# A feed-forward product as seven half-size block products, with the weight sums formed in DRAM

## The chip, the core and the metric

The kernel runs on one core of one Trainium2 chip. Its time is the device time of one execution, in microseconds (us). Names used below: TensorE is PE, VectorE is DVE, ScalarE is ACT, GpSimd is POOL, SyncE is SP. SP issues the weight loads (the hardware queue q1), GpSimd issues the transfers that copy or add from DRAM to DRAM (the software queue q0). All transfers run on the same 16 DMA engines.

## What is computed

One layer of a decoder with D_MODEL = 1024, 512 tokens and D_FF = 2816, all in float32. The parts that matter here:

```python
x = x + rms_norm(merged @ w_out[l], post_mix_g[l])
h = rms_norm(x, pre_ffn_g[l])
gt, up = jnp.split(h @ w_ffn_in[l], 2, axis=-1)      # the first product: (512,1024) @ (1024,5632)
f = (jax.nn.silu(gt) * up) @ w_ffn_out[l]            # the second: (512,2816) @ (2816,1024)
x = x + rms_norm(f, post_ffn_g[l])
```

Before it stand a combined input projection, attention, a pooling mixer and a convolution, whose gated sum is `merged` (the mix).

## The kernel before

Each float32 operand is split into a rounded part (hi, float32r) and the rest (lo), and each product is three matmuls: hi x hi, hi x lo, lo x hi (`mm3`, L1291 to L1295). A "unit" is what one 512 KB weight load feeds. SP loads it into one of three slots of `raw` (L285, L289), once DVE has split the unit three before it. ACT writes `w_hi` (L506; L778 in the second product) once PE has done the unit three before it, DVE writes `w_lo` (L814; L1239), and PE waits for `lo_done`. So every engine goes through the units in one fixed order, written out by hand, and whatever stands between two splits on ACT or DVE delays the next split.

The stages in order of time: the projection with attention (units of 24 matmuls of 512 columns); eight mix units; the output product (`out_tile`, L1472) with the norms and transposes; the first product of the feed-forward part; the second product.

Mix: for each of 8 tiles DVE applies the gates (L1082), GpSimd adds the three branches (L462, L463) for tiles 0 to 6, DVE does it for tile 7 (L1088, L1091), ACT and DVE split the sum (`merged_hi` L674, `merged_lo` L1066). DVE then splits the output weights (`wo_lo_part`). `out_tile(0, 0)` and `out_tile(0, 1)` take steps 0 to 5 first and then steps 6 and 7, each step waiting for its split tile and weights.

First product: 22 tiles of 128 hidden columns, in 11 pairs (tile s and tile s + 11), each tile with a gate unit and an up unit, 44 units (`ff_unit` L1523). The first three units run as two halves of 256 tokens, that is 256 columns a matmul. ACT takes the tanh (L744), DVE makes silu and the product (L1158, L1169, L1175, L1177), and DVE forms for each pair the sums s1 to s4 (L1172 to L1185) that the second product wants.

Second product: it runs as Winograd's form of Strassen's method, seven half-size products in the place of eight (`PH_P1` ... `PH_P4`), in 39 units of 12 matmuls of 512 columns. Four of the seven take sums of weight blocks. GpSimd forms these in DRAM (`combine` L440), a copy and then transfers with an add on landing (L436 and L438), each waiting for the one before it: chunks 0 to 2 early (after the pooling sums), chunks 3 to 5 after the norms. GpSimd's order is: pooling sums, 24 transfers, a power for the layer norm (L457), the mix adds, the norms' reciprocal roots (L467, L391, L395), 24 transfers, the final roots.

Of the kernel before, what the change touches and what calls it, by code (L numbers as in the profile page):

```python
# [29 lines left out]
P = 128  # L30
SEQ = 512
# [25 lines left out]
U_DOWN = U_FF + 2 * FF_TILES  # L57
FF_HALF = FF_TILES // 2
RING = 3
# [9 lines left out]
COMB_STEPS = 8 * COMB_CHUNKS  # L69
DOWN_SPLIT = (PH_P5, PH_P6, PH_P3, PH_P7, PH_P4)  # L70

# [41 lines left out]
def build(nc, x, w_in, w_branch, w_out, w_ffn_in, w_ffn_out, vecs, post_mix_g, pre_ffn_g, post_ffn_g,  # L113
          rel_bias, w_pool_g, onehot, pool_const, out):
    comb = nc.dram_tensor("comb", (4, FF_HALF * P, SEQ), F32, kind="Internal").ap()
    bias_scratch = nc.dram_tensor("bias_scratch", (2 * PAIRS, BIAS_LEN), F32, kind="Internal").ap()
# [54 lines left out]

    a11_hi = at("a11_hi", 68, [FF_HALF, TOK_HALF], F32R)
    a11_lo = at("a11_lo", 79, [FF_HALF, TOK_HALF], F32R)
    a12_hi = at("a12_hi", 90, [FF_HALF, TOK_HALF], F32R)
    a12_lo = at("a12_lo", 101, [FF_HALF, TOK_HALF], F32R)
    s1 = at("s1", 112, [FF_HALF, TOK_HALF])
    s2 = at("s2", 123, [FF_HALF, TOK_HALF])
    s3 = at("s3", 134, [FF_HALF, TOK_HALF])
    s4 = at("s4", 145, [FF_HALF, TOK_HALF])
    n22 = at("n22", 168, [FF_HALF, TOK_HALF])  # L180
    ff_tanh = at("ff_tanh", 156, [2, SEQ])
    ff_silu = at("ff_silu", 160, [2, SEQ])
    ff_prod = at("ff_prod", 164, [2, SEQ])
# [3 lines left out]
    c22 = at("c22", 52, [2, SEQ])  # L187
    c12 = at("c12", 56, [2, SEQ])
    c21 = at("c21", 60, [2, SEQ])
# [16 lines left out]
    with ExitStack() as ctx:  # L206
        bank = [ctx.enter_context(nc.psum_tensor(f"bank{i}", [P, SEQ], F32)) for i in range(8)]

        def sem(name):
# [43 lines left out]
        comb_step, f_mix, s_hi_done, s_lo_done, p_moved, c_made = (  # L253
            sem("comb_step"), sem("f_mix"), sem("s_hi_done"), sem("s_lo_done"), sem("p_moved"), sem("c_made"))
# [7 lines left out]
        w_up_k = w_ffn_in[0].rearrange("(k p) n -> p k n", p=P)  # L262
# [21 lines left out]
        def _(sp):  # L284
# [52 lines left out]
            def ff_load(e, slot):  # L337

                s_, odd = divmod(e, 2)
                col = odd * DFF + (s_ // 2 + FF_HALF * (s_ % 2)) * P  # L340
                load(U_FF + e, slot, w_up_k[:, :, col:col + P], k8)

            for e in range(8):
                ff_load(e, (U_FF + e) % RING)
# [3 lines left out]
            with sp.Fori(0, 3) as i:  # L348
                for jj in range(12):
                    q = jj // 2  # L350
                    col = i * (3 * P) + (jj % 2) * DFF + (2 + q // 2 + FF_HALF * (q % 2)) * P
                    load(U_FF + 8 + i * 12 + jj, (U_FF + 8 + jj) % RING, w_up_k[:, :, bass.ds(col, P)], k8)
# [10 lines left out]
            for n in range(DOWN_UNITS):  # L363
                u = U_DOWN + n
                sp.wait_ge(lo_done, u - RING + 1)
                if n == 5:
                    sp.wait_ge(comb_step, 16 * COMB_STEPS)
# [13 lines left out]
        def _(pool):  # L381
# [45 lines left out]
            comb_count = 0  # L427

            def comb_dma(to, src, rows, add=False):

                nonlocal comb_count
                if comb_count:
                    pool.wait_ge(comb_step, 16 * comb_count)
                comb_count += 1
                if add:
                    pool.dma_start(comb[to, rows, :], src, accum_op=ALU.add).then_inc(comb_step, 16)  # L436
                else:
                    pool.dma_start(comb[to, rows, :], src).then_inc(comb_step, 16)  # L438

            def combine(c):  # L440
# [3 lines left out]
                comb_dma(0, w_ffn_out[0, rows, 0:SEQ], rows)  # L444
                comb_dma(0, w_ffn_out[0, rows, SEQ:], rows, add=True)
                comb_dma(1, comb[0, rows, :], rows)
                comb_dma(1, w_ffn_out[0, low, SEQ:], rows, add=True)
                comb_dma(2, w_ffn_out[0, low, SEQ:], rows)
                comb_dma(2, w_ffn_out[0, rows, SEQ:], rows, add=True)
                comb_dma(3, comb[1, rows, :], rows)  # L450
                comb_dma(3, w_ffn_out[0, low, 0:SEQ], rows, add=True)

            for c in range(3):
                combine(c)
# [3 lines left out]

            for m in range(KT - 1):
                b = m % 2  # L460
                pool.wait_ge(mix_read, m + 1)
# [3 lines left out]
            for t in range(TOK):  # L465
# [25 lines left out]
        def _(act):  # L491
# [254 lines left out]
            for e in range(8):  # L746
                if e >= 1:
                    hi_int(U_FF + 2 + e)
                if e % 2 == 0:
                    j = e // 2  # L750
                    if j:
                        f_hi_part((j - 1) // 2, (j - 1) % 2, j - 1)
                    ff_tanh_part(j, j % 2, FFB[e % 4])
            with act.Fori(0, 3) as i:
                for jj in range(12):
# [891 lines left out]
```

## Time and profile before

| | |
|---|---|
| median of 3 runs | 725.66 us (725.49 to 727.19) |
| profiled execution, its own time | 725.84 us |
| its span, first to last instruction | 724.0 us |
| granted PE clock, mean | 0.997 |
| PE busy | 707.5 us, 98% of the span |
| DVE, ACT, POOL busy | 434.9, 300.6, 88.2 us |
| DMA queues q1 and q0, share of 16 engines | 38.1% and 15.7% |

A busy PE means that a matmul is in flight; matmuls overlap (one of 512 columns is shown 390 ns long and the next starts 227 ns later), so the pace is read from the starts. "Idle before" is the time an engine stood still before an instruction, and the name behind the arrow is what ended it. A DMA is followed from its issue to its landing.

### The profile page before, as it was taken

What the parts mean: (1) busy time and instruction counts of PE and PEld (TensorE: products, weight loads), DVE (VectorE), ACT (ScalarE), POOL (GpSimd) and SP (SyncE); (2) the same over time, 40 slices, a digit from 0 to 9 for tenths busy, and PEclk for the clock granted to TensorE, in tenths of its full rate; (3) what the DMA queues carried; (4) which work ended last, traced back from release to release, by engine and by line L of the source; (5) the groups of instructions that cost most, each with busy time, mean ns of one, the idle gap of its engine ahead of it and who ended that gap; (6) DMA issues with size and microseconds to landing.
All of it is one profiled execution on the core that took longest, in us unless ns stands there. A gap on an engine that the chain in (4) does not pass through costs nothing.

```text
span 724.0 us, 9407 instructions
## 1 busy us (share of the span) xinstructions
PE 707.5 (98%) x3296; PEld 590.6 (82%) x3296; DVE 434.9 (60%) x693; ACT 300.6 (42%) x483; POOL 88.2 (12%) x115
## 2 busy tenths in 40 slices
PE   4999999999999999999999999999999999999996
PEld 4788888888888888888889888888888888888885
DVE  5427868578666575786565445444445444666767
ACT  6324544544455555242443222222222222566653
POOL 2032111111000000760221111111000000000003
PEclk9999999999999999999999999999999999999998
DMA  8436777877623324227327788756232233575563
GB/s 244 118 121 179 174 197 174 196 185 172 170 87 88 89 77 127 88 97 241 99 88 182 200 178 205 184 139 164 88 115 87 88 104 98 176 202 198 183 200 131
DMA packets 123001, 107.32 MB, mean 148 GB/s; under 512 B 4083, under 2 KB 100339, under 8 KB 122780
## 3 DMA queue, kind: packets, MB, share of 16 engines
q1 hardware_dynamic: 114956, 83.86, 38.1%
q0 software_dynamic: 8000, 23.07, 15.7%
q8 instruction: 17, 0.28, 0.1%
q14 instruction: 12, 0.10, 0.0%
q10 hardware_dynamic: 16, 0.02, 0.0%
HBM read 104.82 MB, written 25.19 MB: 180 GB/s over the span
## 4 chain that ended last, share of the span: by engine, by line
PE 95%; DVE 1%; DMA 1%; ACT 1%; POOL 0%; issue 0%; SPq 0%; DVEq 0%; POOLq 0%; ACTq 0%
PE bank L1293 30%; PE bank L1295 30%; PE bank L1294 30%; PE bank L1344 1%; DMA x_tok<-in_x_dram 1%; PE bank L1334 1%; PE bank L1335 1%; PE bank L1361 1%; PE bank L1360 1%; ACT junk L516 0%; DVE x L1113 0%; POOL stat L395 0%; PE bank L1488 0%; DVE xn L1120 0%; PE bank L1351 0%
## 5 line engine op out<-in xcount | busy, mean ns | idle before, releaser
L1293 PE MATMUL bank<-h_hi,w_hi 128*128 128x512 f32 (+1 forms) x712 | 274.1, 385 | 1.8 <-DVE h_lo L842 1.8
L1295 PE MATMUL bank<-h_hi,w_lo 128*128 128x512 f32 (+1 forms) x712 | 272.2, 382 | 0.0
L1294 PE MATMUL bank<-h_lo,w_hi 128*128 128x512 f32 (+1 forms) x712 | 271.9, 382 | 0.0
L814 DVE TENSOR_TENSOR w_lo<-raw,w_hi 128x1024 fp32r<-128x1024 f32 x96 | 121.9, 1270 | 61.7 <-ACT w_hi L506 51.8
L1293 PEld LDWEIGHTS bank<-h_hi,w_hi 128*128 128x128 f32 x712 | 133.9, 188 | 27.4 <-issue 2.2
L1295 PEld LDWEIGHTS bank<-h_hi,w_lo 128*128 128x128 f32 x712 | 133.8, 188 | 26.2
L1294 PEld LDWEIGHTS bank<-h_lo,w_hi 128*128 128x128 f32 x712 | 133.9, 188 | 25.2
L506 ACT ACTIVATE w_hi<-raw 128x1024 fp32r<-128x1024 f32 x88 | 92.7, 1054 | 83.1 <-PE bank L1295 82.9
L1239 DVE TENSOR_TENSOR w_lo<-raw,w_hi 128x1024 fp32r<-128x1024 f32 (+1 forms) x37 | 44.8, 1210 | 29.6 <-ACT w_hi L778 29.5
L778 ACT ACTIVATE w_hi<-raw 128x1024 fp32r<-128x1024 f32 (+1 forms) x37 | 38.8, 1048 | 37.4 <-PE bank L1295 37.4
L1158 DVE SCALAR_TENSOR_TENSOR ff_silu<-ff_tanh,bank 128x512 f32<-128x512 f32 x22 | 15.1, 687 | 61.1 <-ACT ff_tanh L744 61.1
L744 ACT ACTIVATE ff_tanh<-bank 128x512 f32<-128x512 f32 x22 | 13.2, 598 | 87.6 <-PE bank L1295 87.6
L1293 PE MATMUL bank<-w_hi,s_hi 128*128 128x512 f32 x110 | 42.9, 390 | 0.0
L1294 PE MATMUL bank<-w_lo,s_hi 128*128 128x512 f32 x110 | 42.8, 389 | 0.0
L1295 PE MATMUL bank<-w_hi,s_lo 128*128 128x512 f32 x110 | 42.8, 389 | 0.0
L879 DVE SCALAR_TENSOR_TENSOR conv_acc<-u_conv,half_dw,conv_acc 128x512 f32<-128x512 f32 x60 | 41.0, 745 | 0.1
L636 ACT ACTIVATE gate<-bank,half_bias 128x512 f32 (+1 forms) x24 | 16.5, 687 | 47.9 <-PE bank L1295 47.9
L436 POOL DMA_DIRECT2D comb<-in_w_ffn_out_dram x24 | 21.0, 874 | 90.5 <-DMA comb<-in_w_ffn_out_dram 46.3
L482 POOL TENSOR_SCALAR stat<-stat 128x4 f32<-128x4 f32 x1 | 0.3, 307 | 209.4 <-ACT junk L516 209.4
L1293 PE MATMUL bank<-wo_hi,h_hi 128*128 128x512 f32 x64 | 25.1, 392 | 0.0
L1295 PE MATMUL bank<-wo_hi,h_lo 128*128 128x512 f32 x64 | 24.9, 389 | 0.0
L1294 PE MATMUL bank<-wo_lo,h_hi 128*128 128x512 f32 x64 | 24.9, 389 | 0.0
(182 smaller groups left out, 865.7 us busy)
## 6 DMA issues: line engine op xcount, KB each, us to landing
raw<-in_w_ffn_in_dram SPq DMA_DIRECT2D x44, 512.0 KB, 3.9
raw<-in_w_in_dram SPq DMA_DIRECT2D x42, 512.0 KB, 4.2
comb<-in_w_ffn_out_dram POOLq DMA_DIRECT2D x30, 512.0 KB, 5.9
raw<-comb SPq DMA_DIRECT2D x20, 512.0 KB, 3.7
raw<-in_w_ffn_out_dram SPq DMA_DIRECT2D x15, 512.0 KB, 3.7
comb<-comb POOLq DMA_DIRECT2D x10, 512.0 KB, 3.9
raw<-in_w_branch_dram SPq DMA_DIRECT2D x8, 512.0 KB, 3.5
raw<-in_w_out_dram SPq DMA_DIRECT2D x8, 512.0 KB, 3.7
```

The costliest lines, as they stand in the source:

```text
L436: pool.dma_start(comb[to, rows, :], src, accum_op=ALU.add).then_inc(comb_step, 16)
L506: act.activation(w_hi[:, hslot, :], raw[:, slot, :], ACT.Copy).then_inc(hi_done, 1)
L636: act.activation(gate[:, g, :], bank[j % RING][:, :], ACT.Tanh, scale=0.5, bias=half_bias[:, bass.ds(g, 1)]).then_inc(acc_act, 1)
L744: act.activation(ff_tanh[:, b, :], bank[g_bank][:, :], ACT.Tanh, scale=0.5).then_inc(tanh_done, 1)
L778: act.activation(w_hi[:, in_ring(u) % RING, used], raw[:, u % RING, used], ACT.Copy).then_inc(hi_done, 1)
L814: dve.tensor_tensor(dst, src_hi[0], src_hi[1], ALU.subtract).then_inc(lo_done, 1)
L879: dve.scalar_tensor_tensor(out=conv_acc[:, c, :], in0=u_conv[:, c, bass.ds(tap + 2, SEQ)], scalar=half_dw[:, bass.ds(tap + c * CONV_K, 1)] ...
L1158: dve.scalar_tensor_tensor(out=ff_silu[:, b, :], in0=ff_tanh[:, b, :], scalar=1.0, in1=bank[g_bank][:, :], op0=ALU.add, op1=ALU.mult).then ...
L1239: dve.tensor_tensor(w_lo[:, in_ring(u) % RING, used], raw[:, u % RING, used], w_hi[:, in_ring(u) % RING, used].bitcast(F32), ALU.subtract) ...
L1293: pe.matmul(dst, a_hi, b_hi, start=start, stop=False, skip_group_check=resumed)
L1294: pe.matmul(dst, a_hi, b_lo, start=False, stop=False, skip_group_check=resumed)
L1295: return pe.matmul(dst, a_lo, b_hi, start=False, stop=stop, skip_group_check=resumed)
```

## The change

The same method goes to the first product, for 8 of its 11 pairs (`BLOCKS = 8`, `PLAIN = 3`). With the model dimension cut in two halves, the tokens in two halves and the pair in left and right tile, each block takes seven products of a half of the tokens (256 columns) with 4 instead of 8 steps, for gate and up: 7 units of 24 matmuls of 256 columns, where there were 4 units of 24 matmuls of 512. A load is still 512 KB. The host lays out `w_ffn_in` by tile, half and partition, so that a unit is contiguous in each partition.

Four of the seven units take weight sums, which GpSimd forms in DRAM (`comb_up`), 8 transfers a block, 64 in all. GpSimd now keeps two chains side by side (even and odd block or chunk), each transfer waiting for its own chain's last one. Blocks 0 to 5 are formed where chunks 0 to 2 of the second product were. Blocks 6 and 7 come after the layer norm's power and between the mix adds; chunks 0 and 1 between the last mix adds and the norms; chunks 2 to 5 behind the norms.

The sums and differences of the activations' blocks (h11 ... hs4, with their splits) are made by DVE and ACT in the slots of the 12 plain units. PE's results of a block stay in `c_up` (three copies by ACT, three sums by DVE), then tanh, silu and product follow in pieces of 256 tokens. The five operands that the second product wants no longer fit in SBUF: each pair's set (640 KB) is written to DRAM by SP between loads, for pairs 0 to 8, and read back by five DMAs that ACT issues when the last unit of the first product is done; two pairs are moved within SBUF.

```diff
+def block_bank(b, ph):
+    x_bank, z_bank, w_bank = ((0, 1, 4), (5, 6, 2))[b % 2]
+    return {PH_P5: z_bank, PH_P3: z_bank, PH_P2: w_bank}.get(ph, x_bank)
...
+            def block_load(v):
+                b, ph = block_at(v)
...
+                if ph == PH_P5:
+                    sp.wait_ge(up_step[b % 2], 16 * 8 * (b // 2 + 1))
...
+            def spill(kk):
+                sp.wait_ge(f_mix, 4 * kk + 4)
+                sp.dma_start(sets_out[kk], fset[:, kk % 2, 1:6, :]).then_inc(spilled[kk % 2], 16)
...
+            def up_dma(b, to, src, add=False):
+                if up_count[b % 2]:
+                    pool.wait_ge(up_step[b % 2], 16 * up_count[b % 2])
+                up_count[b % 2] += 1
                 if add:
+                    pool.dma_start(comb_up[to, b], src, accum_op=ALU.add, max_dma_last_dim=4096).then_inc(up_step[b % 2], 16)
                 else:
+                    pool.dma_start(comb_up[to, b], src, max_dma_last_dim=4096).then_inc(up_step[b % 2], 16)
...
-            for c in range(3):
-                combine(c)
+            for b in (0, 2, 4):
+                for i in range(8):
+                    up_comb(b, i)
+                    up_comb(b + 1, i)
             pool.wait_ge(ln_dve, 5)
             pool.tensor_tensor(stat[:, 68:72], stat[:, 64:68], stat[:, 88:92], ALU.pow).then_inc(ln_rstd, 1)
+            for i in range(4):
+                up_comb(6, i)
+                up_comb(7, i)
             for m in range(KT - 1):
                 b = m % 2
+                if m < 4:
+                    up_comb(6, 4 + m)
+                    up_comb(7, 4 + m)
+                else:
+                    down_comb(0, m - 4)
+                    down_comb(1, m - 4)
                 pool.wait_ge(mix_read, m + 1)
                 link(pool.tensor_tensor(mix[:, b, 0, :], mix[:, b, 0, :], mix[:, b, 1, :], ALU.add))
...
                 rsqrt(20 + t, 36 + t, 40 + t, 1.0 / D_MODEL, EPS).then_inc(rstd_done, 1)
-            for c in range(3, COMB_CHUNKS):
-                combine(c)
+                down_comb(0, 3 + t)
+                down_comb(1, 3 + t)
+            down_comb(0, 7)
+            down_comb(1, 7)
+            for c in (2, 4):
+                for i in range(8):
+                    down_comb(c, i)
+                    down_comb(c + 1, i)
...
+            def save(b, to, ph):
+                act.wait_ge(unit_done, in_ring(U_BLOCK) + 7 * b + ph + 1)
+                act.activation(c_up[:, b % 2, to, :], bank[block_bank(b, ph)][:, :], ACT.Copy).then_inc(up_saved, 1)
...
+                if n == 2:
+                    act.wait_ge(unit_done, in_ring(U_DOWN))
+                    act.wait_ge(spilled[0], 16 * ((SPILLED + 1) // 2))
+                    act.wait_ge(spilled[1], 16 * (SPILLED // 2))
+                    for i in range(5):
+                        act.dma_start(sets[:, i, 0:SPILLED, :], sets_out[:, :, i, :].rearrange("k p c -> p k c"))\
+                           .then_inc(set_full[i], 16)
...
+            def block_made(b, to, ph):
+                dve.wait_ge(unit_done, in_ring(U_BLOCK) + 7 * b + ph + 1)
+                c = c_up[:, b % 2, to, :]
+                dve.tensor_tensor(c, bank[block_bank(b, ph)][:, :], c, ALU.add).then_inc(up_made, 1)
...
+            def block_unit(b, ph):
+                u = U_BLOCK + 7 * b + ph
+                slot, dst = in_ring(u) % RING, bank[block_bank(b, ph)]
+                for g in range(2):
+                    for k in range(KH):
...
+                        ins = mm3(dst[:, g * TOK_HALF:(g + 1) * TOK_HALF], w_hi[:, slot, ws], w_lo[:, slot, ws], a_hi, a_lo,
+                                  g + k == 0 and ph in DOWN_FIRST, g + k == KH, resumed=True)
+                return ins
...
+                    if ph == PH_P6:
+                        pe.wait_ge(up_saved, 3 * b + 1)
+                    if ph == PH_P3:
+                        pe.wait_ge(up_saved, 3 * b + 2)
+                    if ph == PH_P7:
+                        pe.wait_ge(up_saved, 3 * b + 3)
+                    if ph == PH_P4:
+                        pe.wait_ge(up_made, 3 * b + 2)
```

## Rows read from the trace of the kernel before

**Rows 1.** The page: busy times of the engines; the chain that ended last, by engine.

```profile
PE 707.5 (98%) x3296; PEld 590.6 (82%) x3296; DVE 434.9 (60%) x693; ACT 300.6 (42%) x483; POOL 88.2 (12%) x115
...
PE 95%; DVE 1%; DMA 1%; ACT 1%; POOL 0%; issue 0%; SPq 0%; DVEq 0%; POOLq 0%; ACTq 0%
```

**Rows 2.** Stretches: length; busy us of PE, PEld, DVE, ACT, POOL; PEclk; DMA share; GB/s.

```profile
76.50:79.50 3.00, 3.00 (x19) 2.61 (x18) 2.93 (x10) 1.20 (x3) 0.00 (x0) 1.00 1.06 156
400.00:450.00 50.00, 50.00 (x222) 41.39 (x222) 21.66 (x33) 13.33 (x19) 6.73 (x10) 1.00 0.79 193
450.00:500.00 50.00, 50.00 (x223) 41.39 (x221) 22.82 (x35) 14.11 (x20) 7.28 (x11) 1.00 0.70 170
505.00:545.00 40.00, 40.00 (x178) 33.14 (x177) 18.84 (x29) 10.94 (x16) 0.00 (x0) 1.00 0.31 92
615.00:655.00 40.00, 40.00 (x178) 33.14 (x177) 25.99 (x30) 24.28 (x34) 0.00 (x0) 1.00 0.62 185
```

**Rows 3.** PE in order of time: start us, length us, line, operation; one weight load.

```profile
332.56 0.39 PE L1293 MATMUL bank<-wo_hi,h_hi 128*128 128x512 f32 x1
...
378.54 0.28 PE L1295 MATMUL bank<-h_hi,w_lo 128*128 128x256 f32 x1
...
389.69 0.28 PE L1295 MATMUL bank<-h_hi,w_lo 128*128 128x256 f32 x1
...
391.65 0.39 PE L1295 MATMUL bank<-h_hi,w_lo 128*128 128x512 f32 x1
...
401.85 0.39 PE L1295 MATMUL bank<-h_hi,w_lo 128*128 128x512 f32 x1
...
383.81 0.19 PEld L1295 LDWEIGHTS bank<-h_hi,w_lo 128*128 128x128 f32 x1
```

**Rows 4.** Weight loads issued from 615 to 700, second product.

```profile
DMA to landing us min/median/max: 2.5/3.7/5.6
```

**Rows 5.** DVE: groups of 390 to 715 (busy us, mean ns); two rows in order of time.

```profile
L814 DVE TENSOR_TENSOR w_lo<-raw,w_hi 128x1024 fp32r<-128x1024 f32 x41 | 50.1, 1223 | 5.4 <-ACT w_hi L506 5.2
...
L1218 DVE TENSOR_TENSOR s_lo<-s,s_hi 128x512 fp32r<-128x512 f32 x20 | 13.7, 683 | 0.0
...
L1150 DVE TENSOR_TENSOR a_lo<-ff_prod,a_hi 128x256 f32 x18 | 7.5, 418 | 0.0
...
328.66 0.69 DVE L1091 TENSOR_TENSOR mix<-mix 128x512 f32<-128x512 f32 x1
...
330.66 3.49 DVE L814 TENSOR_TENSOR wo_lo<-raw,wo_hi 128x1024 fp32r<-128x1024 f32 x3
```

**Rows 6.** GpSimd (POOL) in order of time: start us, length us, line, operation.

```profile
185.68 0.88 POOL L436 DMA_DIRECT2D comb<-in_w_ffn_out_dram  x1 [3.50 <-DMA comb<-comb]
...
256.63 1.04 POOL L457 TENSOR_TENSOR stat<-stat 128x4 f32<-128x4 f32 x1 [70.06 <-DVE stat L1027]
...
288.49 2.20 POOL L462 TENSOR_TENSOR mix<-mix 128x512 f32<-128x512 f32 x1 [30.82 <-DVE mix L1082]
...
322.88 2.15 POOL L463 TENSOR_TENSOR mix<-mix 128x512 f32<-128x512 f32 x1
...
375.95 0.69 POOL L438 DMA_DIRECT2D comb<-in_w_ffn_out_dram  x1
...
498.48 0.82 POOL L436 DMA_DIRECT2D comb<-in_w_ffn_out_dram  x1 [2.52 <-DMA comb<-comb]
```

**Rows 7.** DMA queues: packets, MB, share of 16 engines.

```profile
q1 hardware_dynamic: 114956, 83.86, 38.1%
q0 software_dynamic: 8000, 23.07, 15.7%
```

**Rows 8.** One copy on the software queue, issued at 80.9.

```profile
DMA to landing us min/median/max: 3.7/3.7/3.7
```

**Rows 9.** One adding transfer on the software queue, issued at 84.9.

```profile
DMA to landing us min/median/max: 5.6/5.6/5.6
```

**Rows 10.** Weight loads from 390 to 500, beside the software queue.

```profile
DMA to landing us min/median/max: 3.7/4.8/9.4
```

**Rows 11.** Weight loads from 505 to 585, software queue idle.

```profile
DMA to landing us min/median/max: 3.6/3.7/3.8
```

More of the change, by code:

```diff
@@ L56 @@
 FF_TILES = DFF // P
-U_DOWN = U_FF + 2 * FF_TILES
 FF_HALF = FF_TILES // 2
+BLOCKS = 8
+PLAIN = FF_HALF - BLOCKS
+PLAIN_UNITS = 4 * PLAIN
+U_BLOCK = U_FF + PLAIN_UNITS
+BLOCK_UNITS = 7 * BLOCKS
+FF_UNITS = PLAIN_UNITS + BLOCK_UNITS
+U_DOWN = U_FF + FF_UNITS
+KH = KT // 2
 RING = 3
@@ L335, in _, with plain_load @@
                     sp.dma_start(x1[:, 2:4, :], x_tiles[:, 2:4, :]).then_inc(x1_full[1], 16)
[L337 to L344, printed above, removed]
+            def plain_load(v):
+                s_, odd = divmod(v, 2)
+                load(U_FF + v, (U_FF + v) % RING, w_ffn_in[s_ // 2 + FF_HALF * (s_ % 2), :, :, odd, :].rearrange(
+                    "h p c -> p h c"), k2)
@@ new lines, in block_load @@
+            def block_load(v):
+                b, ph = block_at(v)
+                left, right = PLAIN + b, PLAIN + b + FF_HALF
+                if ph == PH_P5:
+                    sp.wait_ge(up_step[b % 2], 16 * 8 * (b // 2 + 1))
+                if ph == PH_P1:
+                    src = w_ffn_in[left, 0]
+                elif ph == PH_P2:
+                    src = w_ffn_in[left, 1]
+                elif ph == PH_P3:
+                    src = w_ffn_in[right, 1]
+                else:
+                    src = comb_up[{PH_P5: 0, PH_P6: 1, PH_P7: 2, PH_P4: 3}[ph], b]
+                load(U_FF + v, (U_FF + v) % RING, src.rearrange("p g c -> p (g c)") if ph in (PH_P1, PH_P2, PH_P3) else src,
+                     lambda tile: tile)
@@ L346, in _ @@
+            def spill(kk):
+                sp.wait_ge(f_mix, 4 * kk + 4)
+                sp.dma_start(sets_out[kk], fset[:, kk % 2, 1:6, :]).then_inc(spilled[kk % 2], 16)
+            for v in range(8):
+                plain_load(v)
             sp.wait_ge(x1_done, TOK)
             sp.dma_start(gain[:, :], bass.AP(post_ffn_g.tensor, 0, [[0, P], [1, D_MODEL]])).then_inc(gain_full, 16)
[L348 to L352, printed above, removed]
+            for v in range(8, FF_UNITS):
+                if v < PLAIN_UNITS:
+                    plain_load(v)
+                else:
+                    block_load(v)
+                if v % 4 == 1 and (v - 9) // 4 < PLAIN:
+                    spill((v - 9) // 4)
+                if v >= PLAIN_UNITS + 16 and (v - PLAIN_UNITS - 16) % 7 == 0 and PLAIN + (v - PLAIN_UNITS - 16) // 7 < SPILLED:
+                    spill(PLAIN + (v - PLAIN_UNITS - 16) // 7)
@@ L451, in combine @@
-                comb_dma(3, w_ffn_out[0, low, 0:SEQ], rows, add=True)
-            for c in range(3):
-                combine(c)
+                if i == 0:
+                    down_dma(c, 0, w_ffn_out[0, rows, 0:SEQ], rows)
+                if i == 1:
+                    down_dma(c, 0, w_ffn_out[0, rows, SEQ:], rows, add=True)
+                if i == 2:
+                    down_dma(c, 1, comb[0, rows, :], rows)
+                if i == 3:
+                    down_dma(c, 1, w_ffn_out[0, low, SEQ:], rows, add=True)
@@ new lines, in down_comb @@
+                if i == 4:
+                    down_dma(c, 2, w_ffn_out[0, low, SEQ:], rows)
+                if i == 5:
+                    down_dma(c, 2, w_ffn_out[0, rows, SEQ:], rows, add=True)
+                if i == 6:
+                    down_dma(c, 3, comb[1, rows, :], rows)
+                if i == 7:
+                    down_dma(c, 3, w_ffn_out[0, low, 0:SEQ], rows, add=True)
+            for b in (0, 2, 4):
+                for i in range(8):
+                    up_comb(b, i)
+                    up_comb(b + 1, i)
@@ new lines, in h_raw_part, with hs_lo_part @@
+            def h_raw_part(dst, k0, t0):
+                part = (slice(k0, k0 + KH), slice(t0, t0 + TOK_HALF))
+                dve.tensor_tensor(dst[:, :, :], h_hi[:, part[0], part[1]].bitcast(F32), h_lo[:, part[0], part[1]].bitcast(F32),
+                                  ALU.add).then_inc(h_raw, 1)
+            def hs_lo_part(i, src, count):
+                dve.wait_ge(hs_hi_done, count)
+                dve.tensor_tensor(hs_lo[:, i, :, :], src[:, :, :], hs_hi[:, i, :, :].bitcast(F32), ALU.subtract)\
+                   .then_inc(hs_lo_done, 1)
@@ L1213, in s_lo_part @@
+            for v in range(FF_UNITS):
+                block_early(v)
+                if v >= 1:
+                    lo_int(U_FF + v + 2)
+                if v <= PLAIN_UNITS:
+                    plain_steps(v)
+                block_steps(v)
             def s_lo_part(n):
```

396 lines of the change are left out of this document (294 added, 102 removed).

## The prediction

> **What bounds the kernel now.** I read the page's busy times and its chain first: TensorE (PE) is busy for 707.5 of 724.0 us and holds 95% of the chain that ended last [rows 1]. So the order is right if PE simply never waits, and time can be won only by giving PE less to do; every other engine and the DMAs count only where they make PE wait. Second, the stretches by stage [rows 2]: in the first product (400 to 585) and in the second one (615 to 655) PE is busy throughout, VectorE (DVE) is at 43 to 65%, and the DMA engines are at 0.31 when only weights are loaded, 0.62 in the second product, and 0.79 and 0.70 while the software queue (GpSimd's) forms the weight sums beside the loads. Third, PE's own pace [rows 3]. Fourth, the software queue and what it does to the loads.
>
> **What the change removes and adds on PE.** 32 of the 44 units of the first product (24 products of 512 columns each) become 56 block units (24 products of 256 columns). In a running stretch 45 products of 512 columns start from 391.65 to 401.85, 0.2267 us each; 93 of 256 columns start from 378.54 to 389.69, 0.1199 us each [rows 3]. Half the columns cost 53%, not 50%. Removed: 32 x 24 x 0.2267 = 174.1 us. Added: 56 x 24 x 0.1199 = 161.1 us. Gain 13.0 us. The price is from the same kind of unit (same operands, same stage), so I give it no range. The seven-for-eight saving alone would be 21.8 us; 8.8 us of it go on the short products. By the Trainium skill, "TensorE: Matmul & The Clock Gate", section "Back-to-back issue gap", the isolated gaps are 262 and 518 cycles, almost in proportion, and the gain would be some 19 us; the row decides against it.
>
> A block unit lasts 24 x 0.1199 = 2.88 us and needs a 512 KB load, a split on ScalarE (ACT) and one on DVE, where a plain unit had 5.44 us for them. The second product already runs at that pace: 12 x 0.2267 = 2.72 us a unit with the same ring of three, and PE is busy 40.00 of 40.00 us [rows 2]. So the ring itself holds, as long as a load lands about as fast as there (3.7 us in the median [rows 4]). DVE's work for a block of seven units (20.1 us) is 7 splits of 1.22, and, counted from the diff, 5 operations of 512 columns at 0.68 and 10 of 256 columns at about 0.42 [rows 5]: 8.6 + 3.4 + 4.2 = 16.2 us, 80%. Tight, but no operation of it has to be ready in less than one unit, and splits run two units ahead. I price it at 0 and up to 2 us. The twelve extra sums and splits of the activations in the plain units cost DVE about 15 us in ten units of 5.44 us in which it is 43% busy [rows 2]: hidden, 0.
>
> **The software queue.** Before, it forms sums in 48 transfers (40 of 512 KB, 8 of 256 KB, which is 44 full ones), each waiting for the one before: 24 of them until 192, 24 more from 375.95 to 502 [rows 6]. They hold the 16 engines for 15.7% of 724 us = 114 us, or 2.6 us each [rows 7]. A copy lands in 3.7, an adding transfer in 5.6 us [rows 8, 9]; with the mean of 2.6 and that difference of 1.9, a copy holds the engines 1.6 and an adding one 3.5 us (estimate). In a stretch in the middle of an adding one the DMA share is 1.06, and no load gets in [rows 2]. The change adds 64 transfers, 32 x (1.6 + 3.5) = 163 us of engine time, and puts them in two chains side by side. It also adds 24 loads (some 40 us at 0.31 x 5.44 = 1.7 us each), nine spills of 640 KB and five reloads of 1.2 MB (some 37 us at the same rate). The 16 engines go from 15.7% + 38.1% = 53.8% of the span [rows 7] to (390 + 240)/724 = 87%.
>
> First part, 48 transfers from 55.8 until the norm's reciprocal root at 256.63 [rows 6]: engine time 122 us, and beside loads at 0.31 there is room for 0.69 x 200.8 = 139 us. It fits with 17 us to spare, and PE has 16.3 us for a ring of three there. Price 0, but the margin is small.
>
> **The mix stage.** Here GpSimd adds the branches: it is released for tile m at 288.49 + 5.44 m, works 3.9 us, and rests 1.5 us in each period; its last one ends at 325.03 [rows 6]. The change puts two DMA issues ahead of each (0.7 or 0.8 us apiece), each behind a wait for its chain's previous transfer. Queued behind those waits are the adds; behind the adds wait ACT and DVE (splitting merged tiles, then the output weights), then PE. With the engines serving one software transfer at a time, two copies need 3.7 + 1.6 = 5.3 us from the first issue to the last landing, two adding ones 5.6 + 3.5 = 9.1 us, and each more beside a load. Tile by tile: m = 0 and 1 are on time; m = 2 must see both adding transfers of m = 1 (issued at about 292 and 293) land, at 302, and ends at 307 (before 303.3); m = 3 ends at 313, m = 4 at 318 (its transfers open two new chains and wait for nothing); m = 5 waits for copies that stand behind the adding ones of m = 3, ends at 327.5; m = 6 waits for the adding ones of m = 5, ends at 336, that is 11 us late. DVE's last add has 328.66 - 325.03 = 3.6 us of slack, and PE needs the result (last split of 330.66 on, first split out at 331.9) at 332.56, 0.6 us of slack [rows 3, 5]. PE stops for 11 - 3.6 - 0.6 = 6.8 us. Bounds: 0 if the two chains do not slow each other (each then as quick as the single one; m = 6 ends at 328, within the slack), 12 if a transfer needs 0.3 us more each time. I take 7, because the share of 1.06 says that they do slow each other. In the norm stage behind it, two issues (2 us) stand in GpSimd's gaps; I add 1 (0 to 2).
>
> **The block stage.** At its start (before: 390 + 9 x 5.44 = 439; now some 7 later) the software queue has about 34 transfers less 18 done = 16 to go, half of them of 256 KB, some 35 us of engine time. Loads want 1.7 of each 2.88 us and the spills 0.1 more, together 0.68. Beside one chain, loads landed in 4.8 us in the median and 9.4 at most, against 3.7 alone [rows 10, 11]. A ring of three at 2.88 us allows 8.6 - 1.1 - 1.2 - 0.2 = 6.1 us. Lower bound 0 to 1: software transfers use only the third that is left. Upper bound: turns, one load, one software transfer, 1.7 + 2.6 = 4.3 us per unit until 35/2.6 = 14 transfers are through, 14 x 1.4 = 20 us. I take 8, nearer the middle, since the chains pause at each landing. By the Trainium skill, "DMA: Bandwidth & Descriptors", section "Queues, rings and completion order", an engine goes round the queues that have work, a packet at a time; that speaks for the turns, and by it alone the sum would be 12 us worse. The trace agrees in part: the load that took 9.4 us.
>
> **The second product.** Five reloads go out from ACT when the last block unit is done (five issues, each at most the 0.69 us that one takes GpSimd [rows 6], 3.5 us of ACT's time in a stage where it is 61% busy [rows 2]), 19 us of engine time beside loads that take 0.62. The first is needed five units (13 us) on. 0 if loads get their share, 9 if they stand behind whole reloads. I take 2.
>
> **The sum** against the profiled execution (725.84 us, 1.84 around its span, 0.18 above the median of 725.66): 725.8 - 13.0 + 7 + 1 + 8 + 2 = 730.8. I forecast 731.
>
> **The rivals.**
> A, covered (the other side): the waits are short, and the software transfers fit in the gaps. For it: PE never waited beside one chain at 0.79. Against: GpSimd's 1.5 us gap. Stalls of 1 + 0 + 2 + 0: 716. It decides if tile 6 of the mix ends before 330. Chance 0.30.
> B, stalls cancel the gain: mix 7, norm 1, block 4, second product 1: 726. Chance 0.13.
> C, my forecast, 728 to 736: 0.39.
> D, the DMA engines are the bound: turns in the block stage (18), whole reloads in front of loads (6), mix 7 to 10, norm 1: 745 to 748. For it: 87% of the span. Chance 0.16.
> E, the change does not do what it says: block products are paced by their weight loads, each shown at 0.19 us [rows 3], instead of by their columns at 0.12. 1344 x 0.07 = 94 us more. The first six half units already ran at 0.12. Chance 0.02.
>
> **How the numbers follow.** A measurement of this kernel can tell 0.3% (2.2 us) from nothing: under 723.5 is faster, over 727.8 slower. Faster 0.31 (A and the low edge of B), same 0.12, slower 0.57. The range 714 to 747 holds A, B, C and most of D.
>
> **What would show it.** PE's spacing in block units 0.120 us. PE's idle time by stage: a gap of some 7 us between the mix units and the sixth step of the output product, released by DVE; the adds of GpSimd late by 4 us at tile 2 and 11 at tile 6, each behind a DMA. In the first half of the block stage gaps released by w_lo, loads landing at 6 us or more and a DMA share near 1; none in its second half. If GpSimd's tile 6 ends by 328, the step on the mix stage is wrong; if PE is busy through the block stage while the software queue works, the step on turns is.

## The result, and the profile after

| | before | changed |
|---|---|---|
| median, same chip | 725.88 us (725.49 to 727.19, 4 runs) | 737.34 us (734.9 to 740.99, 4 runs) |
| profiled execution, its span | 725.84, 724.0 us | 736.5, 734.6 us |
| granted PE clock, mean | 0.997 | 0.991 |

The change makes the kernel slower: the ratio is 1.016 [1.0137 to 1.0183], 11.5 us where 5.2 were forecast. The side was right and the range held, but the loss is more than double.

The page of the changed kernel, against [rows 1, 7]:

```profile
PE 700.7 (95%) x3872; PEld 610.6 (83%) x3872; DVE 483.3 (66%) x761; ACT 343.9 (47%) x545; POOL 126.9 (17%) x179
...
q1 hardware_dynamic: 81820, 102.34, 42.6%
q0 software_dynamic: 17216, 56.63, 33.3%
q10 hardware_dynamic: 7168, 7.23, 3.0%
...
PE 73%; DMA 14%; DVE 4%; ACT 2%; POOL 2%; ACTq 2%; issue 1%; SPq 0%; DVEq 0%; POOLq 0%
```

PE's share of the chain fell from 95% to 73%, and DMA's rose from 1% to 14%: PE now waits for data. To see where, I read PE's timeline and took three stages from it: "out", from the first product of `wo_hi` to the last transpose of `xn`; "first", from there to the first product on `a_hi`; "second", from there to the start of the last product but one. In us, profiled executions:

| | out | first | second |
|---|---|---|---|
| before | 324.40 to 378.19: 53.8 | to 612.88: 234.7 | to 717.43: 104.6 |
| changed | 324.14 to 382.30: 58.2 | to 611.71: 229.4 | to 727.93: 116.2 |
| difference | +4.4 | -5.3 | +11.7 |

By the forecast of PE's gain the first product would last 234.7 - 13.0 = 221.7 without waits, so 7.7 of it are waits. The three places are now read one by one.

**Out stage.** The changed kernel, first PE, then DVE, then GpSimd, each in order of time (start us, length us, line, operation, idle time before it and what ended that). The first line of GpSimd is the layer norm's power; it belongs to an earlier stage and is used further below:

```profile
332.07 0.39 PE L1614 MATMUL bank<-wo_hi,h_lo 128*128 128x512 f32 x1
334.95 0.62 PE L1612 MATMUL bank<-wo_hi,h_hi 128*128 128x512 f32 x1 [2.49 <-DVE wo_lo L1028]
335.36 0.63 PE L1613 MATMUL bank<-wo_lo,h_hi 128*128 128x512 f32 x1
335.79 0.63 PE L1614 MATMUL bank<-wo_hi,h_lo 128*128 128x512 f32 x1
```
```profile
331.59 0.69 DVE L1305 TENSOR_TENSOR mix<-mix 128x512 f32<-128x512 f32 x1 [4.12 <-POOL mix L599]
...
333.58 3.49 DVE L1028 TENSOR_TENSOR wo_lo<-raw,wo_hi 128x1024 fp32r<-128x1024 f32 x3
```
```profile
256.36 1.04 POOL L583 TENSOR_TENSOR stat<-stat 128x4 f32<-128x4 f32 x1 [46.52 <-DVE stat L1241]
...
324.40 0.55 POOL L554 DMA_DIRECT2D comb<-comb  x1 [3.46 <-DMA comb<-in_w_ffn_out_dram]
328.28 0.52 POOL L554 DMA_DIRECT2D comb<-comb  x1 [3.33 <-DMA comb<-in_w_ffn_out_dram]
328.81 1.30 POOL L598 TENSOR_TENSOR mix<-mix 128x512 f32<-128x512 f32 x1
330.19 1.29 POOL L599 TENSOR_TENSOR mix<-mix 128x512 f32<-128x512 f32 x1
```

Read from below: GpSimd waited 3.46 us for a landing, issued, and waited 3.33 us for another, so its last add ended at 331.5 instead of 325.03 [rows 6]; DVE's tile 7 starts at 331.59 instead of 328.66 [rows 5], `wo_lo` at 333.58 instead of 330.66, and PE starts 2.88 us after its last product instead of 0.227. Then the products start 0.43 us apart instead of 0.227: the granted clock is at its lower level, 1.2 GHz, from 335.1 to 338.5. Eight products at that pace cost another 1.7 us. Together 4.3 of the 4.4.

**Block stage.** Stretches, with the columns of [rows 2]; the waits of ACT from 440 to 530 (us in total, times, longest); weight loads of 440 to 520, then of 520 to 600; PE around one stop, and two of its products from the later part; ACT ahead of that stop:

```profile
446.00:526.00 80.00, 74.75 (x612) 73.48 (x611) 49.24 (x72) 37.69 (x52) 13.07 (x18) 1.00 0.96 283
526.00:606.00 80.00, 79.57 (x664) 79.40 (x663) 61.19 (x90) 42.22 (x60) 0.00 (x0) 1.00 0.64 222
```
```profile
ACT w_hi L648 <- DMA raw<-comb_up: 22.2, 11, 4.3
ACT w_hi L648 <- DMA raw<-in_w_ffn_in_dram: 15.6, 8, 5.6
```
```profile
DMA to landing us min/median/max: 4.0/7.5/10.0
...
DMA to landing us min/median/max: 3.0/3.3/5.8
```
```profile
491.72 0.28 PE L1614 MATMUL bank<-hs_hi,w_lo 128*128 128x256 f32 x1
493.32 0.36 PE L1612 MATMUL bank<-hs_hi,w_hi 128*128 128x256 f32 x1 [1.32 <-ACT c_up L915]
...
559.75 0.28 PE L1614 MATMUL bank<-hs_hi,w_lo 128*128 128x256 f32 x1
...
564.19 0.28 PE L1612 MATMUL bank<-hs_hi,w_hi 128*128 128x256 f32 x1
```
```profile
490.84 1.06 ACT L648 ACTIVATE w_hi<-raw 128x1024 fp32r<-128x1024 f32 x1 [3.29 <-DMA raw<-comb_up]
...
492.59 0.59 ACT L915 ACTIVATE c_up<-bank 128x512 f32<-128x512 f32 x1
```

While the software queue works, the DMA engines are at 0.96, a load lands 7.5 us after its issue in the median, ACT waits 37.8 us for loads and PE loses 5.3 of 80 us, in stops of up to 1.75 us. The stop shown is ended by ACT's copy of a result, `c_up`, which stands in ACT's order behind a split that had waited 3.29 us for its load. When the queue is done, loads land in 3.3 us and PE loses 0.4 of 80. The last two lines of PE are 37 products apart: 0.1200 us each, as priced.

**Second product.** ACT, PE and DVE at its start, the stretch, and what the reloads' queue (q10) moved from 612 to 640:

```profile
611.97 1.06 ACT L982 ACTIVATE w_hi<-raw 128x1024 fp32r<-128x1024 f32 x1 [1.82 <-PE bank L1614]
612.25 2.04 ACTq L989 DMA_DIRECT2D sets<-sets_out  x2
...
614.31 11.85 ACTq L989 DMA_DIRECT2D sets<-sets_out  x3
626.26 1.06 ACT L982 ACTIVATE w_hi<-raw 128x1024 fp32r<-128x1024 f32 x1 [12.45 <-issue]
```
```profile
619.67 0.39 PE L1614 MATMUL bank<-w_hi,a_lo 128*128 128x512 f32 x1
628.63 0.79 PE L1612 MATMUL bank<-w_hi,a_hi 128*128 128x512 f32 x1 [8.57 <-DVE w_lo L1557]
629.22 0.63 PE L1613 MATMUL bank<-w_lo,a_hi 128*128 128x512 f32 x1
```
```profile
627.35 1.23 DVE L1557 TENSOR_TENSOR w_lo<-raw,w_hi 128x1024 fp32r<-128x1024 f32 x1 [12.13 <-ACT w_hi L982]
```
```profile
612.00:632.00 20.00, 11.43 (x44) 9.03 (x43) 7.14 (x13) 5.80 (x9) 0.00 (x0) 0.83 1.02 331
```
```profile
q10 hardware_dynamic: 5840, 5.90, 65.6%
```

ACTq is the issuing of DMAs. The five reload issues took 2.04 + 11.85 = 13.9 us of ACT (one by one 0.42, 1.59, 3.82, 4.65, 3.31), 2.8 us each in place of the 0.69 that I had allowed. The next weight split stood behind them: "12.45 <-issue". DVE waited for that split, and PE for DVE: 8.96 us from one product to the next, of which 8.7 are lost. Behind it the products are again 0.43 us apart, and the granted clock is at 1.2 GHz from 625.2 to 632.1 (about 1.7 us lost). One more stop of 1.21 us stands at 649.20. Together 11.4 of the 11.7.

### The profile page after: what moved, and what is told of

The parts are those of the page before. It is cut to its first block, busy times and chain, and to the rows that moved or that the text cites. A ratio compares the mean times of both kernels' runs of the same rounds, so it can differ in the third digit from the quotient of the medians.

```text
span 734.6 us, 10445 instructions
## 1 busy us (share of the span) xinstructions
PE 700.7 (95%) x3872; PEld 610.6 (83%) x3872; DVE 483.3 (66%) x761; ACT 343.9 (47%) x545; POOL 126.9 (17%) x179
## 3 DMA queue, kind: packets, MB, share of 16 engines
q1 hardware_dynamic: 81820, 102.34, 42.6%
q0 software_dynamic: 17216, 56.63, 33.3%
## 4 chain that ended last, share of the span: by engine, by line
PE 73%; DMA 14%; DVE 4%; ACT 2%; POOL 2%; ACTq 2%; issue 1%; SPq 0%; DVEq 0%; POOLq 0%
PE bank L1612 23%; PE bank L1614 23%; PE bank L1613 23%; DMA raw<-in_w_ffn_in_dram 4%; DMA raw<-comb_up 3%; DMA comb<-in_w_ffn_out_dram 2%; DMA raw<-comb 2%; ACTq L989 2%; DMA comb_up<-in_w_ffn_in_dram 2%; DVE w_lo L1028 1%; PE bank L1663 1%; ACT w_hi L648 1%; DMA x_tok<-in_x_dram 1%; PE bank L1653 1%; PE bank L1654 1%
## 5 line engine op out<-in xcount | busy, mean ns | idle before, releaser
L1028 DVE TENSOR_TENSOR w_lo<-raw,w_hi 128x1024 fp32r<-128x1024 f32 x120 | 148.8, 1240 | 108.8 <-ACT w_hi L648 99.0
L1612 PE MATMUL bank<-h_hi,w_hi 128*128 128x512 f32 (+1 forms) x584 | 211.2, 362 | 3.6 <-DVE w_lo L1028 1.8
L1614 PE MATMUL bank<-h_hi,w_lo 128*128 128x512 f32 (+1 forms) x584 | 209.1, 358 | 0.0
L1613 PE MATMUL bank<-h_lo,w_hi 128*128 128x512 f32 (+1 forms) x584 | 208.9, 358 | 0.0
L1612 PE MATMUL bank<-hs_hi,w_hi 128*128 128x256 f32 x320 | 91.3, 285 | 3.9 <-ACT c_up L915 1.3
L1613 PE MATMUL bank<-hs_lo,w_hi 128*128 128x256 f32 x320 | 90.7, 283 | 0.0
L1614 PE MATMUL bank<-hs_hi,w_lo 128*128 128x256 f32 x320 | 90.7, 283 | 0.0
L1612 PEld LDWEIGHTS bank<-hs_hi,w_hi 128*128 128x128 f32 x320 | 61.5, 192 | 4.9 <-DVE w_lo L1028 3.1
L1613 PEld LDWEIGHTS bank<-hs_lo,w_hi 128*128 128x128 f32 x320 | 61.5, 192 | 0.0
L1614 PEld LDWEIGHTS bank<-hs_hi,w_lo 128*128 128x128 f32 x320 | 61.5, 192 | 0.0
```

The lines of the kernel that those rows point to most:

```text
L1028: dve.tensor_tensor(dst, src_hi[0], src_hi[1], ALU.subtract).then_inc(lo_done, 1)
L1612: pe.matmul(dst, a_hi, b_hi, start=start, stop=False, skip_group_check=resumed)
L1613: pe.matmul(dst, a_hi, b_lo, start=False, stop=False, skip_group_check=resumed)
L1614: return pe.matmul(dst, a_lo, b_hi, start=False, stop=stop, skip_group_check=resumed)
```

## The experiments

The theory: three separate stops, each at its own place, whose sizes add up. (1) GpSimd's adds queue behind DMA waits; (2) two chains of software transfers crowd the loads; (3) the five reloads hold up the second product. The rival: one cause, the DMA engines as a whole are full (D of the prediction), so that what is won at one place is lost at the next. The ratios are all to the kernel before, from the same chip; the changed kernel's is 1.016 [1.0137 to 1.0183]. Stages are read from one profiled execution of each kernel.

**spread.** The reloads apart in time, each when its turn in the second product nears.

```diff
-                    for i in range(5):
-                        act.dma_start(sets[:, i, 0:SPILLED, :], ...)
+                if n in (2, 6, 10, 14, 18):
+                    i = (n - 2) // 4
+                    act.dma_start(sets[:, i, 0:SPILLED, :], ...)
```

> The changed kernel, with one edit: ACT issues the five reloads of the sets one at a time, at steps 2, 6, 10, 14 and 18 of the second product, and not all five at step 2. The bytes are the same. In the changed kernel the five issues took 0.42, 1.59, 3.82, 4.65 and 3.31 us, PE stood still for 8.96 us and ran at the lower clock level for 6.8 us after it. Theory 1 (the issues hold ACT because its queue is full, and with ACT the weight splits): every issue under 1 us, no stop and no low clock there, the time 10 to 11 us lower, some 726 us. Rival (the reloads' bytes hold up the weight loads): the stop stays at 4 us or more in smaller pieces, the time falls by 5 us or less.

Measured: 731.79 us (730.45 to 735.07), ratio 1.0087 [1.0053 to 1.0121]. Second product 106.1 us in place of 116.2. ACT's reload issues:

```profile
618.75 0.42 ACTq L990 DMA_DIRECT2D sets<-sets_out  x1
...
629.57 0.37 ACTq L990 DMA_DIRECT2D sets<-sets_out  x1
...
662.78 0.37 ACTq L990 DMA_DIRECT2D sets<-sets_out  x1
```

The same five issues cost 0.37 to 0.42 us each when one at a time is in flight. So 0.4 us is the price of an issue, and the rest was waiting for those before it. That is the 10 us expected of this stage, but the median fell by 5.5 only. In the profiled execution the first product was 4.1 us longer (233.5) than in the changed kernel's and the out stage 2.3 (60.5), though the edit acts only behind them. Those two stages vary between executions of kernels that are the same up to there, as the table below shows; that the other three executions lost it in the same places isn't shown.

**poolissue.** The burst stays, but GpSimd issues it, which is idle there. With that it also goes over the software queue and no longer over ACT's hardware queue.

```diff
+            pool.wait_ge(unit_done, in_ring(U_DOWN))
...
+            for i in range(5):
+                pool.dma_start(sets[:, i, 0:SPILLED, :], ...).then_inc(set_full[i], 16)
             def final_rstd(t):
```

> The changed kernel, with one edit: GpSimd issues the five reloads, all at once at the end of the first product; ACT issues none. The burst of 5.9 MB stays. Theory 1 (only ACT's time matters): no stop of ACT, the time 9 to 11 us lower. Rival (the burst fills the DMA engines, weight loads stand behind it): loads land in 8 us or more, PE still stops for 4 us or more in the first ten units of the second product, and the time falls by less than 7 us.

Measured: 736.85 us (733.76 to 741.84), ratio 1.0163 [1.0112 to 1.0214]: no gain. GpSimd, then the weight loads from 612 to 634, then ACT and PE at a stop:

```profile
614.76 5.05 POOL L621 DMA_DIRECT2D sets<-sets_out  x5 [95.52 <-PE bank L1614]
```
```profile
DMA to landing us min/median/max: 4.7/10.0/13.6
```
```profile
631.53 1.06 ACT L989 ACTIVATE w_hi<-raw 128x1024 fp32r<-128x1024 f32 x1 [3.08 <-DMA raw<-comb]
```
```profile
634.60 0.47 PE L1612 MATMUL bank<-w_hi,s_hi 128*128 128x512 f32 x1 [1.44 <-DVE s_lo L1537]
```

This is the run that taught most. ACT was free, and still the second product lasted 114.5. In place of one stop of 9 us there are six, of which one is shown, of 1.0 to 2.6 us, 9.3 us over the pace in sum. The loads landed in 10.0 us in the median and as late as 13.6; in the changed kernel it was 6.7 from 612 to 634. So the burst of 5.9 MB between loads is enough for the loss, with ACT held or free. What isn't shown is how much a burst on ACT's own queue would cost if it did not hold ACT: no run separates that from the change of queue.

**clear.** No DMA wait among the mix adds: for each of the blocks 6 and 7, six of the eight transfers go ahead of the layer norm's power, where GpSimd waited 46.52 us. The rest go straight behind it, with the first three for each of chunks 0 and 1; the fourth ones go behind the mix.

```diff
+            for i in range(6):
+                up_comb(6, i)
+                up_comb(7, i)
+
             pool.wait_ge(ln_dve, 5)
...
             for m in range(KT - 1):
                 b = m % 2
-                if m < 4:
-                    up_comb(6, 4 + m)
-                    up_comb(7, 4 + m)
-                else:
-                    down_comb(0, m - 4)
-                    down_comb(1, m - 4)
                 pool.wait_ge(mix_read, m + 1)
```

> The changed kernel, with one edit in GpSimd's order: no DMA between the adds of the mix. Twelve of the transfers for blocks 6 and 7 go before the layer norm's power (GpSimd waited 46.5 us there), the rest and the first six for chunks 0 and 1 between it and the mix, two behind the mix. Theory (adds queued behind waits for DMAs): GpSimd's adds are on time as before the change (last one done at 325), no stop at the output product and no low clock there, 4 to 5 us lower, some 732. Rival (the stop comes from loads that land late, not from the adds): the stop stays. A second risk: the power for the layer norm is late, which PE would show as a gap near 257 us.

Measured: 734.03 us (732.71 to 735.35), ratio 1.012 [1.01 to 1.014]. The out stage lasts 53.8, as before, and GpSimd's adds are back at their old times:

```profile
321.41 1.68 POOL L599 TENSOR_TENSOR mix<-mix 128x512 f32<-128x512 f32 x1 [1.53 <-DVE mix L1298]
323.17 2.15 POOL L600 TENSOR_TENSOR mix<-mix 128x512 f32<-128x512 f32 x1
```

**nosw.** The sums of chunks 2 to 5 are left out, 32 transfers, and the second product loads plain weights in their place, so the result of the layer is another. That leaves the software queue empty in the block stage.

> The changed kernel without the 32 transfers that form the weight sums of chunks 2 to 5 of the second product, which then takes plain weight blocks in their place: this part of the result is left out. From 385 us on the software queue is idle. Theory (turns with the software queue make PE wait in the block stage): the six stops of 7.3 us in all between 450 and 530 vanish, loads land in 4 us, the time is 6 to 7 us lower, some 730. Rival (the ring or DVE at 2.88 us a unit, or the spills, are too slow by themselves): stops of 3 us or more stay in the block stage.

Measured: 729.48 us (727.11 to 730.09), ratio 1.0043 [1.0027 to 1.0059]. The stretch, and its loads (440 to 520):

```profile
448.00:528.00 80.00, 80.00 (x669) 80.00 (x668) 56.82 (x80) 41.72 (x58) 0.00 (x0) 1.00 0.68 216
```
```profile
DMA to landing us min/median/max: 3.2/4.2/5.5
```

PE is busy all through. The first product lasts 221.9 us, against 234.7 before: 12.8 us of gain, where 13.0 were priced, and DVE at 71% of the stretch costs nothing. Of the 7.7 us, 7.5 are the software queue's doing (229.4 - 221.9).

**serial.** All the sums are formed, but chunks 4 and 5 with one transfer in flight at a time.

```diff
-            for c in (2, 4):
+            for i in range(8):
+                down_comb(2, i)
+                down_comb(3, i)
+            for c in (4, 5):
                 for i in range(8):
+                    pool.wait_ge(comb_step[(c + 1) % 2], 16 * down_count[(c + 1) % 2])
                     down_comb(c, i)
-                    down_comb(c + 1, i)
```

> The changed kernel, with one edit in GpSimd's order: the 16 transfers of chunks 4 and 5, those that run beside the block stage, go one at a time and not two side by side. The work is the same. Without any transfers there the stops of the block stage were gone (run nosw). Theory (it is the second transfer in flight that makes a load wait twice): stops in the block stage fall from 7 us to 2 us or less, the last transfer ends near 550 and still before its first use near 630, the time is 4 to 6 us lower, some 732. Rival (the sum of the work decides, in whatever order): the stops stay at 5 us or more, spread over a longer time.

Measured: 733.87 us (729.65 to 734.95), ratio 1.0099 [1.0068 to 1.013]. First product 225.5, that is 3.8 us of waits in place of 7.7; loads of 440 to 520 land in 5.6 us in the median, in place of 7.5. The same bytes, only not two at a time: that took away half of the loss. 3.8 lies between the two expectations (2 or less, 5 or more). One at a time the last transfer is also issued later, at 577 instead of 514, so the number in flight and the lower rate aren't told apart.

**spread_clear** and **all3.** The first two cures together, then with the third.

> Two edits together: reloads one at a time (as in spread) and no DMA between the mix adds (as in clear). Theory (the three stops are separate): 737.3 - 10.8 (the stop and the low clock at the second product) - 4.3 (the same at the output product) = some 722, with the block stage's stops left, which differ by some us from run to run. That would be faster than the kernel before the change (725.8). Rival (what is won at one place is lost in the crowd behind it): above 726.

Measured: 722.63 us (717.32 to 726.75, 10 runs), ratio 0.9962 [0.9938 to 0.9986]. That is as expected, and more than the two alone had given: 2.0% off the changed kernel's ratio, where spread gave 0.7% and clear 0.4%. In eight of the ten executions the granted clock was 0.994 or more, in those of the changed kernel, spread and clear 0.987 to 0.993, so long stops had become rarer. The profiled one (726.06) is one of the other two.

> Three edits together: reloads one at a time, no DMA between the mix adds, chunks 4 and 5 one transfer at a time. Theory: all three stops are small, PE's work alone is left: 725.8 - 13.0 = 712.8 and up to 4 us of small waits, 713 to 717. Rival (the engines are the bound at 87 to 90% of their time): above 720.

Measured: 720.2 us (719.13 to 722.05), ratio 0.9932 [0.9912 to 0.9952]. This missed the expected 713 to 717 and fell on the rival's side of 720. By stage the rest is 3.7 us in the first product (225.5 against 221.7) and 3.7 in the second (108.3 against 104.6). Nor do the gains cancel, for the time is below both spread's and clear's; but the interval overlaps that of spread_clear, so what the third cure adds to the time isn't shown. Whether the rest is a bound or more stops, fine has to tell.

**six.** all3 with 6 blocks in place of 8: 16 software transfers, 6 loads and the sums of two pairs less, and 3.2 us less of PE's gain.

> all3 with six blocks and not eight: 20 plain units and 42 block units, sixteen software transfers and six loads fewer. PE's work rises by 2 x (13.0/8) = 3.25 us. Theory (with the stops mostly gone each block is worth 1.6 us of PE): 3 us above all3, less what the lighter DMA load gives back, 721 to 724. Rival (DMA engines bound the eight-block version): six blocks are as fast as eight or faster, 720 or less.

Measured: 721.75 us (720.36 to 725.09, 10 runs), ratio 0.9948 [0.9933 to 0.9962]. If the engines as a whole were the bound, this lighter kernel would be the faster one. It isn't, though the intervals overlap. Its first product lasts 225.1, where 234.7 - 9.75 = 224.9 is what PE needs; its second one, with the same reloads as all3, is no shorter (109.0 and 108.3). But the first product of all3, with two blocks more, lasts 225.5: there the 3.25 us that the last two blocks save on PE went into waits.

**fine** and **fine_half.** fine is all3 with each reload in three parts of some 400 KB, 15 issues spread over the units; fine_half also halves the transfers of chunk 4.

```diff
+                parts = (2, 3, 4, 5, 7, 9, 11, 13, 15, 17, 19, 21, 23, 25, 27)
+                if n in parts:
+                    i, j = divmod(parts.index(n), 3)
+                    ks = slice(3 * j, 3 * j + 3)
+                    act.dma_start(sets[:, i, ks, :], ...)
```

> all3 with one edit: each reload is cut into three (fifteen of 0.4 MB in the place of five of 1.2 MB), issued over steps 2 to 27 of the second product. In all3 the second product still took 3.8 us more than before the change, in five stops of 0.5 to 1.05 us. Theory (a weight load stands behind the whole of a reload, so a third of the length costs less than the ring's slack): its stage within 1 us of the kernel before (104.6 us), the time 2 to 3 us below all3, some 717.5. Rival (the bytes decide): no change.

Measured: 715.76 us (713.79 to 720.0), ratio 0.9849 [0.9831 to 0.9866].

> fine with one more edit: chunk 4's eight software transfers are cut in halves (256 KB as those of chunk 5 are), sixteen, still one at a time. Theory (the length of the one software transfer that a load waits for decides): the block stage falls from 3.8 us above its bare work to 2 or less, 716 or so. Rival (the work decides, and a fixed cost per transfer comes on top): no gain or a small loss against fine, and the last software transfer ends later.

Measured: 714.88 us (713.99 to 717.04), ratio 0.9859 [0.9836 to 0.9883]. Stretches of its block stage and second product:

```profile
440.00:520.00 80.00, 80.00 (x668) 79.96 (x667) 56.75 (x81) 40.88 (x56) 7.25 (x11) 1.00 0.88 261
520.00:600.00 80.00, 80.00 (x668) 79.96 (x667) 59.07 (x87) 41.80 (x61) 8.86 (x13) 1.00 0.82 253
600.00:700.00 100.00, 99.11 (x437) 81.54 (x436) 71.96 (x89) 61.32 (x89) 2.80 (x5) 1.00 0.78 254
```

PE is busy 259.1 of 260 us with the DMA engines at 0.88, 0.82 and 0.78. The parts of the reloads are worth 0.8% beyond all3, with intervals that do not touch; whether the halved transfers add anything stays open. The profiled execution of fine is the slowest of its five (720.0): its first product has a stop of 2.57 us at 498.61 and the low clock from 500.9 to 504.3. Both kernels are faster than before by some 10 us and than the changed one by over 20, and they do the same arithmetic and form the same sums as the changed one. 725.84 - 13.0 = 712.8 would be the time without any wait; 2 us of that are left to win.

All the profiled executions by stage, in the order of cures:

| | out | first | second |
|---|---|---|---|
| before | 53.8 | 234.7 | 104.6 |
| adds behind DMA waits (changed, spread, poolissue, nosw, serial) | 58.2, 60.5, 58.2, 60.0, 60.2 | | |
| adds clear (clear, spread_clear, all3, six, fine, fine_half) | 53.8 in each | | |
| two chains (changed, spread, poolissue, clear, spread_clear) | | 229.4, 233.5, 231.9, 229.9, 232.4 | |
| chunks 4 and 5 one at a time (serial, all3, fine; fine_half) | | 225.5, 225.5, 228.1; 222.0 | |
| no transfers there (nosw); six blocks (six) | | 221.9; 225.1 | |
| burst of reloads (changed, clear, nosw, serial; poolissue) | | | 116.2, 116.0, 115.0, 116.5; 114.5 |
| five reloads apart (spread, spread_clear, all3, six) | | | 106.1, 107.5, 108.3, 109.0 |
| fifteen parts (fine, fine_half) | | | 105.2, 106.0 |

The first and the last column follow their own edit and no other. The middle one does so with a wider spread: fine (228.1) stands nearer to the two-chain kernels than to its own row. That is the evidence that three causes were at work, and not one.

## Why the prediction was right or wrong

**PE's gain, -13.0: right.** 12.8 us without the software queue, 0.1200 us a product. Rival E is out.

**The Trainium skill on the gaps** (a gain of some 19 us, estimated from "TensorE: Matmul & The Clock Gate", "Back-to-back issue gap"): the trace of the changed kernel does not agree. The two sizes stayed at 0.120 and 0.227 us.

**First part and DVE, 0: right.** GpSimd had 46.52 us to spare before the norm's root, more than the 17 us of engine time that I had counted. The 48 transfers ran from 55.8 to some 210 us, 154/48 = 3.2 us each. The queues took 42.6 + 33.3 + 3.0 = 79% of the engines' span, not 87%: I had priced a software transfer at a mean of 2.6 us, and for the changed kernel this was too high by about a seventh (33.3% of 734.6 us over 64 + 44 transfers is 2.3). That makes some 4 of the 8 points.

**The mix stage, 7 (0 to 12): right in mechanism, 4.4 in size (up to 6.7 in other executions).** Every link was there: transfer, add, tile 7, split, PE. But the delay did not grow tile by tile as I had worked it out: tile 2 ended at 303.7, 0.5 us late and not 4, tile 5 at 320.9, 1.4 late, and nearly all came at once in the two waits ahead of tile 6. That ended at 331.5 and not at 336, and PE stopped for 2.7 us and not 6.8. What I had left out is the low clock behind the stop, 1.7 us. Two errors of opposite sign. The norm stage, 1: 0.

**The block stage, 8 (0 or 1 to 20): right,** 7.7 us in this execution and 7.7 to 11.8 in the five two-chain ones. The signs were those named: stops only while the software queue works, loads above 6 us, a DMA share near 1 (0.96). The name of what ends a stop was not always the `w_lo` that I had named, as the one shown tells. One sum in it was off: 16 transfers, half of them half as big, are 12 full ones, at 2.6 us 31 us and not 35. By the Trainium skill's rule of turns ("DMA: Bandwidth & Descriptors", "Queues, rings and completion order") it would have been 12 us more, as the prediction worked it out. The loads' 7.5 us against 4.2 without the software queue agree with turns in kind; in size the trace stands well below.

**The second product, 2 (0 to 9): the step that failed.** It cost 11.7, outside its bounds, and that is the whole surprise: with 2 here, the time would have been 727. Two things went wrong. The price of the issues was taken from a row of GpSimd, 0.69 us, and called "at most", though the same group of rows has issues of 0.82 and 0.88 [rows 6]; behind each other the five took 2.8 us each on ACT. And "the first is needed five units on" was only asked of the reloads. What mattered was what stands between: the loads of those five units had to pass 5.9 MB that held the engines for 18.4 us (65.6% of 28 us). The estimate of 19 us of engine time was right; the choice of 2 between 0 and 9 had no row behind it. poolissue shows the upper end, 9 for whole reloads in front of loads, to be about right (9.9, on the other queue); in the changed kernel 1.7 us of low clock came on top.

**The sum:** -13.0 + 4.4 + 0 + 7.7 + 11.7 - 0.2 for what lies around = +10.6 of span (734.6 - 724.0). The stages before came out 4 us cheaper than their 16. That hides part of the 9.7 us missed in the second product, and is luck: by their prices and its 11.7 the time would have been 740 to 741. In spread, nosw and serial the out stage alone cost 6.2 to 6.7.

**The rivals.** A fell at its own test (tile 6 before 330: 331.5). B and C had the right order of sizes in the first two places, but the time lies above both, and below D (745 to 748). D had 6 us for whole reloads in front of loads, nearer to what came than my 2. Its ground, that the engines are the bound, is wrong: with the same bytes fine takes 715.76, so the engines can carry all of it; they were full only in stretches, and there because of the order and the size of the transfers.

**What stays open.** Why the block stage with two chains costs 7.7 in one execution and 11.8 in another. A part is the clock: the four stops of the changed kernel there are 1.16 to 1.75 us long and it never falls; in spread two of the stops are 3.95 and 2.07 us long, the clock is low for 3.4 us behind each, and products of 256 columns start 0.213 us apart in place of 0.120, which makes about 3 of the 4.1 us between the two. Why the waits gather into longer stops in one execution isn't shown. And when the clock falls: behind stops of 2.88, 3.86, 3.95 and 2.07 us it did, behind one of 3.11 us (poolissue, at 460.13) it did not.

## What to carry to other kernels

Ask of every burst of DMAs not only when its own data is needed but which small loads have to pass it, and cut it up so that each piece fits in the slack of one unit; here that turned 11.7 us of the second product into 0.6 to 1.4. Keep an in-order engine that others wait for free of waits on slow transfers: the same transfers, issued some places earlier in GpSimd's order, cost nothing. And when a change saves little per unit and makes the stage tighter, price the stops, not the bytes: the bytes fitted from the start.

## What the runs showed of the hardware

- A DMA issue on ACT takes 0.37 to 0.42 us when no reload is in flight, and 1.6 to 4.7 us behind others of 1.2 MB; the instructions behind it wait. GpSimd issued the same five, on the software queue, in 5.05 us, 1.0 each.
- A stop of PE has a tail. Behind the stop of 2.88 us the granted clock was at 1.2 GHz for 3.4 us, behind that of 8.96 us for 6.8 us (10.2 behind similar stops in clear, serial and nosw), and products of 512 columns started 0.43 us apart in place of 0.227.
- Beside the burst of reloads the engines were full: from 612 to 632 the DMA share was 1.02, and reloads and weight loads together moved at 331 GB/s.
